# Hybrid decoder layer on one core: resident shared-expert weights, moved routing tables, merged list products

## The chip, the cores and the metric

The kernel runs on one core of a Trainium2 chip. Its time is the device time of one execution in microseconds (us); lower is better. The engines are PE (TensorE, matrix products into PSUM), DVE (VectorE), ACT (ScalarE), POOL (GpSimd) and SP (SyncE, which issues most transfers). All transfers run on 16 DMA engines that the queues of SP, ACT and POOL share.

## The reference

One decoder layer for 512 tokens of width 1024, all in f32. After the token mixers the layer computes a shared expert and 8 of 64 routed experts for each token:

```python
h2 = rmsnorm(x, g_ffn)
idx, wts = route(h2, w_router, router_bias)   # sigmoid scores, top 4 of 8 groups, top 8 of 64 experts
moe = routed_experts(h2, idx, wts, w_exp_gate, w_exp_up, w_exp_down) \
    + swiglu(h2, w_sh_gate, w_sh_up, w_sh_down)
x = x + moe
x = x + sigmoid(rmsnorm(x, g_ple) @ w_ple_gate) * rmsnorm(p @ w_ple_proj, g_ple_post)
```

`swiglu(x, wg, wu, wd)` is `(silu(x @ wg) * (x @ wu)) @ wd`. Gate and up weights, shared or of one expert, are 1024 x 256 (1 MiB each), down weights 256 x 1024 (1 MiB).

## The kernel before, in words

**Memory.** `ring` has 12 slots of 8 KB for each partition, 1 MiB each. It holds the dense weights of the mixers first (`DENSE`, `DENSE_SLOT`), then the experts: the four experts of a group take three slots each, from slot 9, 0, 3 and 6 on (`EXPERT_SLOT`; gate, up, down). `gates` holds the mixers' gates, 16 chunks of 512; once the branches are merged into its first half `lo`, the second half `hi` is free. Before the change `hi` then takes the gain row `gffn`, the per-layer inputs `prow`, the router weights `rw` and the scratch of the selection (`choice`, `masked`, `repl`, `gscr`).

**Stages.** Query, key, value and pool products, attention and gates run to 208 us; the two branches and their merge to 265 us; the output projection, second norm, router and selection of the four 128-token tiles interleave from 263 to 349 us (PE's order is written out by hand: `out_proj`, `second_T`, `router`, `rank`, with pieces of `shared_up` as filler); then 40 row steps to 909 us; then the rows are summed and the last gate applied.

**Row steps.** A list of (token, expert) pairs is built for each group of four experts: `place` is a one-hot matrix of list slots, bf16, made by DVE (`places`). PE multiplies it with two tables: `tokc` (token index in two exact bf16 parts, `list_rows`, 2 columns wide) and `tokw` (three bf16 parts of the weight and the rank, 4 columns for each of two experts, `list_weights`, 8 columns wide). Groups 0 to 7 have lists of 96 rows for each expert and take three steps of 128 rows, groups 8 to 15 have 64 and take two. The lists of group r are made in step r, for r from 1 to 15, between the row transposes and the down product; the weights of group 0 join in step 1.

A step r is on PE: gate and up products of 128 gathered rows (L2105, four strips of 32 rows with an expert each), transposes of the activations of step r-1 (L2114), transposes of the rows of step r+1 (`rows_T`, L1654), `lists(r)`, then the down product of step r-1 (L2134). POOL gathers rows from `h2_rows` in HBM and scatters weighted results to `accumulator`, 0.5 MiB each way for a full step. The first gather waits until all of `h2_rows` is stored by ACT's queue (L900), and until the first row list is there. PE's order before the first step is: two pieces of a shared product, `rows_T(0)`, the last four k of `shared_up(1)`, then `up(0)`.

**SP's queue.** Loads are issued in program order, each behind a wait for its slot. `load_group(g)` loads group g while group g-1 is computed: gate and up of position 0 after step 0 of the group, of position 1 after step 1, of positions 2 and 3 after step 2 (L500), and the down weights behind the down products (L519). In front of the loop stand the weights of experts 0 to 3; gate and up of expert 3 are the last, after `shared_ps` has reached 2.

**The shared expert.** `shared_up` computes gate and up of tiles 0 and 1 ahead of the loop, from ring slots 6 and 7. Those slots are then needed for expert 3, so the same weights are loaded a second time, into pieces of `gates` (`shg_late`, `shu_late`, L547 and L549), for tiles 2 and 3, which are computed in steps 24 to 26 (`late_up`: eight products 256 wide for gate and eight for up). SP issues the second load after the first gather has landed (L546).

## Time and profile before

| | |
|---|---|
| time, median of 3 runs (lowest to highest) | 996.4 us (994.88 to 996.63) |
| profiled execution: its time, its span | 995.38 us, 993.5 us |
| busy: PE, DVE, ACT, POOL | 941.1, 339.4, 162.6, 201.4 us |
| moved by DMA | 301.03 MB, 303 GB/s over the span |
| mean granted TensorE clock | 0.986 of full |

Some times of the profiled execution around the change, from its timeline: SP issued gate and up of expert 2 at 327.5 us; DVE ended the last gain product at 330.3; ACT issued the last store of h2 rows at 332.3; DVE ended the last masked weights at 336.5; POOL issued the first gather at 338.8; SP issued gate and up of expert 3 at 349.6; PE began the first row step at 349.3. The transfers that SP issued from 343.4 to 371.2 are, in order: the shared gate (1 MiB), the shared up in two halves (1 MiB), the post gain (0.5 MiB), gate and up of expert 3 (2 MiB), gate and up of position 0 of group 1 (2 MiB), the two halves of the per-layer projection (1 MiB), gate and up of position 1 (2 MiB) and the down weights of position 0 (1 MiB).

How to read it: the span runs from the first to the last instruction, the execution's time is some 2 us longer. Busy times overlap between engines. An idle engine costs something only where the chain runs through it.

### The profile page before, as it was taken

To read this page: it belongs to the slowest core of one execution; us is meant where nothing else is said; L and a number is where in the kernel's file an instruction comes from. 1 tells how busy PE (TensorE), PEld (TensorE's weight loads), DVE (VectorE), ACT (ScalarE), POOL (GpSimd) and SP (SyncE) were. 2 spreads that over 40 slices of the span, in tenths; PEclk is the share of its full clock that TensorE was granted. 3 is DMA by queue.
4 is the path that set the end of the run, shared out by engine and by line. 5 is a ranking of instruction groups with operands and counts; after the bars stand their busy time and mean duration, and the time that the engine had idled before them with its cause. 6 is when DMAs were issued, how large, how long until landed. Compare 5 with 4: busy or idle time off the path is not lost.

```text
span 993.5 us, 15496 instructions
## 1 busy us (share of the span) xinstructions
PE 941.1 (95%) x6263; PEld 465.7 (47%) x6263; DVE 339.4 (34%) x749; ACT 162.6 (16%) x304; POOL 201.4 (20%) x332
## 2 busy tenths in 40 slices
PE   6999999999999999999999999999979898997698
PEld 4578888854446533333333333354323332332344
DVE  5565673222226753333332111111101111111687
ACT  2001334120011211111111111111101112121021
POOL 4115923000010102222222222212121211101210
PEclk9999999999999999999999999999989999999799
DMA  9940002265362599999999999999999999999972
GB/s 331 326 128 1 1 1 85 85 201 180 105 288 75 195 385 373 410 416 401 393 418 415 414 419 414 410 423 415 405 422 422 422 420 421 414 400 361 368 274 84
DMA packets 83911, 301.03 MB, mean 303 GB/s; under 512 B 9299, under 2 KB 35959, under 8 KB 59648
## 3 DMA queue, kind: packets, MB, share of 16 engines
q1 hardware_dynamic: 71200, 264.24, 67.7%
q0 software_dynamic: 11920, 33.63, 8.7%
q10 hardware_dynamic: 720, 2.16, 0.5%
q8 instruction: 50, 0.82, 0.3%
q14 instruction: 21, 0.17, 0.0%
HBM read 279.26 MB, written 29.36 MB: 311 GB/s over the span
## 4 chain that ended last, share of the span: by engine, by line
PE 76%; DMA 18%; DVE 2%; SPq 2%; issue 1%; ACT 1%; DVEq 0%; POOL 0%; ACTq 0%
PE ps L2105 22%; DMA ring<-in_w_exp_up 16%; PE ps L1721 12%; PE ps L2134 9%; PE ps L1860 6%; PE ps L2247 5%; PE ps L1677 3%; PE ps L1844 3%; PE ps L1842 3%; PE ps L1654 2%; DMA ring<-in_w_exp_down 2%; PE ps L1931 1%; PE ps L1683 1%; PE ps L2114 1%; SPq L514 1%; SPq L500 1%
## 5 line engine op out<-in xcount | busy, mean ns | idle before, releaser
L2105 PE MATMUL ps<-ring,gates 128*32 128x512 f32 x2560 | 288.8, 603 | 26.1 <-DMA ring<-in_w_exp_up 25.4
L2105 PEld LDWEIGHTS ps<-ring,gates 128*32 128x32 f32 x2560 | 87.6, 111 | 219.0 <-issue 218.1
L2134 PE MATMUL ps<-ring,poolbuf 128*32 128x512 f32 x1280 | 147.3, 601 | 3.0 <-DMA ring<-in_w_exp_down 2.1
L1482 DVE COPY poolbuf<-ps 128x256 f32<-128x256 f32 x40 | 17.0, 424 | 356.2 <-PE ps L2114 356.2
L747 POOL TENSOR_TENSOR tickets<-cst 128x1 f32<-128x1 f32 x77 | 14.5, 188 | 398.2 <-ACT actT L946 392.7
L2134 PEld LDWEIGHTS ps<-ring,poolbuf 128*32 128x32 f32 x1280 | 38.3, 110 | 84.7 <-issue 83.0
L946 ACT ACTIVATE actT<-ps,qT 128x1024 f32<-128x1024 f32 x40 | 44.5, 1113 | 143.9 <-PE ps L2134 143.9
L938 ACT ACTIVATE poolbuf<-ps 128x256 f32<-128x256 f32 x40 | 15.3, 384 | 279.3 <-PE ps L2105 279.3
L1721 PE MATMUL ps<-xrow,ring 128*128 128x256 f32 x256 | 57.9, 381 | 0.1
L1860 PE MATMUL ps<-ring,gates 128*128 128x512 f32 x128 | 56.4, 594 | 0.0
L1654 PE MATMUL ps<-cst,rows 128*128 128x128 f32 x352 | 48.5, 285 | 7.6 <-DVE rows L1035 7.6
L1721 PEld LDWEIGHTS ps<-xrow,ring 128*128 128x128 f32 x256 | 48.3, 190 | 8.0 <-issue 1.2
L1654 PEld LDWEIGHTS ps<-cst,rows 128*128 128x128 f32 x352 | 44.7, 193 | 9.5 <-issue 8.9
L1721 PE MATMUL ps<-actT,ring 128*128 128x256 f32 x208 | 47.5, 381 | 0.0
L688 POOL TENSOR_SCALAR st<-st 128x1 f32<-128x1 f32 (+2 forms) x17 | 6.7, 393 | 196.2 <-ACT rows L891 135.3
L759 POOL DMA_INDIRECT rows<-h_rows,stage x40 | 41.8, 1045 | 21.4 <-issue 19.0
L764 POOL DMA_INDIRECT accumulator<-actT,stage x40 | 40.6, 1016 | 22.1 <-issue 22.1
L2247 PE MATMUL ps<-ring,actT 128*128 128x512 f32 (+1 forms) x112 | 42.2, 531 | 0.0
L1721 PEld LDWEIGHTS ps<-actT,ring 128*128 128x128 f32 x208 | 39.0, 190 | 6.7 <-issue 1.4
L720 POOL TENSOR_TENSOR ring<-ring 128x1024 f32<-128x1024 f32 x12 | 28.3, 2361 | 52.4 <-DMA ring<-in_w_gate 30.3
L1860 PEld LDWEIGHTS ps<-ring,gates 128*128 128x128 f32 x128 | 23.8, 190 | 27.3 <-issue 27.3
L2247 PEld LDWEIGHTS ps<-ring,actT 128*128 128x128 f32 x112 | 20.9, 190 | 18.0 <-issue 17.2
(269 smaller groups left out, 1001.3 us busy)
## 6 DMA issues: line engine op xcount, KB each, us to landing
ring<-in_w_exp_down SPq DMA_DIRECT2D x64, 1024.0 KB
ring<-in_w_exp_gate SPq DMA_DIRECT2D x62, 1024.0 KB, 10.8
ring<-in_w_exp_up SPq DMA_DIRECT2D x62, 1024.0 KB, 18.9
ring<-accumulator SPq DMA_DIRECT2D x12, 1024.0 KB, 12.5
ring<-in_w_gate SPq DMA_DIRECT2D x8, 1024.0 KB, 10.1
ring<-in_w_in SPq DMA_DIRECT2D x5, 1024.0 KB, 13.0
xrow<-in_x SPq DMA_DIRECT2D x8, 512.0 KB, 7.5
accumulator<-ring SPq DMA_DIRECT2D x1, 4096.0 KB, 19.6
```

The source lines that it names most:

```text
L759: pool.indirect_dma_start(hg[j], None, h2_dram, bass.IndirectOffsetOnAxis(ap=stage[:, 0, j, :], axis=0), bounds_check=T - 1, oob_is_err=Fa ...
L764: pool.indirect_dma_start(y_dram, bass.IndirectOffsetOnAxis(ap=stage[:, 1, j, :], axis=0), yrow[j], None, bounds_check=ACC_ROWS - 1, oob_i ...
L946: nc.scalar.activation(yrow[j], bank(6, 2), ACT.Copy, scale=slot_wr[:, r, 0:1]).then_inc(y_ready, 1)
L1654: last = nc.tensor.transpose(bank(b0 + half)[:, k * width:(k + 1) * width], v[0:width, 4 * half + k, :], ident[0:width, 0:width])
L1677: last = mm(bank(2 * (i % 2)), actT[:, k, i * P:(i + 1) * P], qv[:, k], start=(k == 0), stop=(k == KD - 1))
L1721: last = mm(out[:, f * HALF_T:(f + 1) * HALF_T], w[:, k, f * P:(f + 1) * P], x[:, k, :], start=(k == 0), stop=(k == 3))
L1842: mm(bank(b), wa[:, k, mi * P:(mi + 1) * P], mixedT[:, k, :], start=(k == 0), stop=(k == 3))
L1844: last = mm(bank(b + 1), wb[:, k, mi * P:(mi + 1) * P], qT[:, k, :], start=(k == 0), stop=(k == 3))
L1860: last = mm(bank(half), gates[:, k, i * P:(i + 1) * P], w[:, k], start=(k == 0), stop=(k == KD - 1))
L2105: last = mm(bank(2 + k)[part, :], hgT[k][:, q, part], pair_view(EXPERT_SLOT[js[c]])[:, q], start=(q == 0), stop=(q == KD - 1))
L2134: last = mm(bank(6 + half)[part, :], eactT[r % 2][:, q, part], w[:, q, half * 512:(half + 1) * 512], start=(q == 0), stop=(q == 1))
L2247: last = mm(gate_bank(i, n0)[:, 0:width], xT, unit_view(s, 4)[:, k % 4, n0 % 512:n0 % 512 + width], start=(k == 0), stop=(k == KD - 1))
```

## The change

The first load of the shared gate and up weights goes into all of `hi` (`w_sh`), behind the routing tables, and stays there for all four tiles; the second load is gone. The routing tables take ring slots 6 and 7: `gffn` and `prow` slot 6, `rw` and the selection's scratch slot 7. So expert 3's gate weights (slot 6) are loaded once the gain products and the transposes of `prow` are done, and its up weights (slot 7) once the selection's masked weights are there; neither waits for the first gather or for `shared_ps`. `gpost` is loaded ahead of both. The shared activations `sh_row` move to the last quarter of `lo`.

`tokw` gets six columns for each expert: the two of `tokc`, copied in once, and the four it had. One product of 12 columns (`list_all`) takes the place of `list_rows` and `list_weights`; only the first list of group 0 is still made from `tokc` alone (`first_rows`). `late_up` makes eight products 512 wide. An unused identity copy (`idT`) is dropped.

```diff
@@ -53,7 +53,8 @@
 TCOL, WCOL = 2, 4
-LCOL = TCOL + 2 * WCOL
+ECOL = TCOL + WCOL
+LCOL = 2 * ECOL
 LATE = (2, 3)
@@ -148,8 +149,8 @@
 DENSE = ["q0", "q1", "kv", "pool0", "pool1"] + [f"gate{p + h * PAIRS}" for p in range(PAIRS) for h in range(2)] + \
-    ["wa0", "wb0", "wa1", "wb1"] + [f"out{c}" for c in range(4)] + ["shg", "shu"]
-DENSE_SLOT = [u % 8 for u in range(17)] + [1, 2, 3, 4, 6, 7]
+    ["wa0", "wb0", "wa1", "wb1"] + [f"out{c}" for c in range(4)]
+DENSE_SLOT = [u % 8 for u in range(17)] + [1, 2, 3, 4]
 DENSE_AT = {name: n for n, name in enumerate(DENSE)}
@@ -224,19 +225,17 @@
         pp = hi.rearrange("p (i n) -> p i n", i=NT)
-        prow = hi[:, 2 * D:3 * D].rearrange("p (i n) -> p i n", i=NT)
-        rw = hi[:, 3 * D:3 * D + KD * NE].rearrange("p (k e) -> p k e", k=KD)
-        gffn = hi[:, 0:D]
-        sh_row = hi[:, 0:NT * FE].rearrange("p (i f) -> p i f", i=NT)
+        gffn = ring[:, 6, 0:D]
+        prow = ring[:, 6, D:2 * D].rearrange("p (i n) -> p i n", i=NT)
+        rw = ring[:, 7, 0:KD * NE].rearrange("p (k e) -> p k e", k=KD)
+        w_sh = hi.rearrange("p (u k n) -> p k u n", u=2, k=KD)
+        sh_row = lo[:, 3 * D:4 * D].rearrange("p (i f) -> p i f", i=NT)
         sh_act = hi[:, 2 * T:4 * T].rearrange("p (j n) -> p j n", j=2)
...
         NR = NT * NE
-        lo3 = lo[:, 3 * D:4 * D]
         rows3 = rows[:, 3, :]
-        shg_late = hi[:, 2 * D:4 * D].rearrange("p (k n) -> p k n", k=KD)
-        shu_late = [w.rearrange("p (k n) -> p k n", k=KD // 2) for w in (lo3, hi[:, D:2 * D])]
-        choice, masked, repl, gscr = (hi[:, D + k * NR:D + (k + 1) * NR] for k in range(4))
+        choice, masked, repl, gscr = (ring[:, 7, KD * NE + k * NR:KD * NE + (k + 1) * NR] for k in range(4))
         key_row, above, perm = (poolbuf[0:NE, PL + k * NE:PL + (k + 1) * NE] for k in range(3))
@@ -250,7 +249,7 @@
         ka = kT[:, :, :].rearrange("p a n -> p (a n)")
-        WM = NR * WCOL // 2
+        WM = NR * ECOL // 2
         tokw = ka[:, 0:WM].bitcast(BF16).rearrange("p (i e c) -> p i e c", i=NT, e=NE)
@@ -264,7 +263,6 @@
         oneT = sb("oneT", [P, P], BF16)
-        idT = sb("idT", [P, P], BF16)
         order = vecs[0:1, 0:NE].bitcast(U32)
@@ -313,7 +311,7 @@
         x1_ps, x1_ready = sem("x1_ps"), sem("x1_ready")
-        mid_loaded, late_loaded, sh_late_loaded = sem("mid_loaded"), sem("late_loaded"), sem("sh_late_loaded")
+        mid_loaded, late_loaded, shared_loaded = sem("mid_loaded"), sem("late_loaded"), sem("shared_loaded")
         ssq2_done, rstd2_ready, xg_ready, h2_ready, act_moved = (
@@ -369,10 +367,6 @@
                 return t["w_out"][0].rearrange("(k p) n -> p k n", p=P)[:, :, n * 256:(n + 1) * 256]
-            if name == "shg":
-                return t["w_sh_gate"][0].rearrange("(k p) n -> p k n", p=P)
-            if name == "shu":
-                return t["w_sh_up"][0].rearrange("(k p) n -> p k n", p=P)
             raise ValueError(name)
@@ -481,18 +475,19 @@
             sp.dma_start(y_rows[0], zero_row.unsqueeze(1).broadcast_to([P, TOPK, D])).then_inc(y_first, 16)
-            for u in range(8, DENSE_AT["shg"]):
+            for u in range(8, N_DENSE):
                 load_dense(u)
...
                 sp.dma_start(xrow[:, i, :], x_rows[i]).then_inc(x_loaded[i], 16)
-            for u in range(DENSE_AT["shg"], N_DENSE):
-                load_dense(u)
             sp.wait_ge(merged_ready, KD)
...
             sp.dma_start(rbias, t["router_bias"].broadcast_to([P, NE])).then_inc(mid_loaded, 16)
+            for u, name in enumerate(("w_sh_gate", "w_sh_up")):
+                sp.dma_start(w_sh[:, :, u, :], t[name][0].rearrange("(k p) n -> p k n", p=P)
+                             ).then_inc(shared_loaded, 16)
@@ -540,16 +535,13 @@
             load_in(2, 2)
+            sp.dma_start(gpost, t["g_ple_post"].broadcast_to([P, D])).then_inc(late_loaded, 16)
+            sp.wait_ge(xg_ready, 2 * NT)
+            sp.wait_ge(pT_ps, 2)
+            load_part(3, 3, 0)
             sp.wait_ge(logit_ps, NT)
-            sp.wait_ge(pT_ps, 2)
-            sp.wait_ge(sel_ready, NT)
-            sp.wait_ge(gathered[0], 16)
-            sp.dma_start(shg_late, unit_source("shg")).then_inc(sh_late_loaded, 16)
-            for c in range(2):
-                sp.dma_start(shu_late[c], unit_source("shu")[:, 4 * c:4 * c + 4, :]).then_inc(sh_late_loaded, 16)
-            sp.dma_start(gpost, t["g_ple_post"].broadcast_to([P, D])).then_inc(late_loaded, 16)
-            sp.wait_ge(shared_ps, 2)
-            load_in(3, 3)
+            sp.wait_ge(masked_ready, 2)
+            load_part(3, 3, 1)
             sp.wait_ge(order_ready, 1)
@@ -1055,7 +1047,6 @@
             nc.vector.memset(oneT[:, :], 1.0)
-            nc.vector.tensor_copy(idT[:, :], cst[:, C_ID:C_ID + P])
@@ -1310,6 +1301,10 @@
             nc.vector.tensor_copy(tokc[:, :, 1], cst[:, C_TILE:C_TILE + NT])
+            nc.vector.tensor_copy(tokw[:, :, :, 0],
+                                  cst[:, C_PM:C_PM + 1].unsqueeze(1).broadcast_to([P, NT, NE]))
+            nc.vector.tensor_copy(tokw[:, :, :, 1],
+                                  cst[:, C_TILE:C_TILE + NT].unsqueeze(2).broadcast_to([P, NT, NE]))
             residual(0, 0)
@@ -1409,11 +1404,11 @@
             tw3 = tokw.rearrange("p i e c -> p (i e) c")
-            link(nc.vector.tensor_copy(tw3[:, :, 0], r_w))
-            link(nc.vector.tensor_tensor(rest, r_w, tw3[:, :, 0], ALU.subtract))
-            link(nc.vector.tensor_copy(tw3[:, :, 1], rest))
-            link(nc.vector.tensor_tensor(rest, rest, tw3[:, :, 1], ALU.subtract))
-            nc.vector.tensor_copy(tw3[:, :, 2], rest)
+            link(nc.vector.tensor_copy(tw3[:, :, TCOL], r_w))
+            link(nc.vector.tensor_tensor(rest, r_w, tw3[:, :, TCOL], ALU.subtract))
+            link(nc.vector.tensor_copy(tw3[:, :, TCOL + 1], rest))
+            link(nc.vector.tensor_tensor(rest, rest, tw3[:, :, TCOL + 1], ALU.subtract))
+            nc.vector.tensor_copy(tw3[:, :, TCOL + 2], rest)
@@ -1424,7 +1419,7 @@
                 b, span = 1 - b, 2 * span
-            nc.vector.tensor_scalar(tokw[:, :, :, 3], count_of[:, b, :, HEAD:], -1.0, None, ALU.add
+            nc.vector.tensor_scalar(tokw[:, :, :, TCOL + 3], count_of[:, b, :, HEAD:], -1.0, None, ALU.add
                                     ).then_inc(tokw_ready, 1)
@@ -1434,7 +1429,7 @@
                 r = slice(FIRST_STEP[g], FIRST_STEP[g] + n)
-                w = found[:, :, TCOL:].rearrange("p s (e c) -> p s e c", e=2)
+                w = found.rearrange("p s (e c) -> p s e c", e=2)[:, :, :, TCOL:]
                 own = cst[:, C_PAIR:C_PAIR + 6] if g < BIG_GROUPS else cst[:, C_PAIR2:C_PAIR2 + 4]
@@ -1909,26 +1904,17 @@
-                i = LATE[c]
-                pe.wait_ge(sh_late_loaded, 48)
                 pe.wait_ge(h2T_ready, 2 * NT + 2 * c + 2)
                 for k in range(KD):
-                    xT = xT_late[k // 4][:, k % 4, :]
-                    mm(bank(5)[:, 0:FE], xT, shg_late[:, k, :], start=(k == 0), stop=(k == KD - 1))
-                for k in range(KD):
-                    xT = xT_late[k // 4][:, k % 4, :]
-                    last = mm(bank(5)[:, FE:2 * FE], xT, shu_late[k // 4][:, k % 4, :], start=(k == 0),
-                              stop=(k == KD - 1))
+                    last = mm(bank(5), xT_late[k // 4][:, k % 4, :], w_sh[:, k], start=(k == 0), stop=(k == KD - 1))
                 last.then_inc(shared_ps, 1)
...
                 if i == 0 and k0 == 0:
-                    loaded("shg")
-                    loaded("shu")
-                w = pair_view(DENSE_SLOT[DENSE_AT["shg"]])
+                    pe.wait_ge(shared_loaded, 32)
                 for k in range(k0, k1):
-                    last = mm(bank(SH_BANK[i]), actT[:, k, i * P:(i + 1) * P], w[:, k], start=(k == 0),
+                    last = mm(bank(SH_BANK[i]), actT[:, k, i * P:(i + 1) * P], w_sh[:, k], start=(k == 0),
                               stop=(k == KD - 1))
@@ -1982,13 +1968,14 @@
-            def list_rows(g, at, s):
+            def first_rows(at, s):
                 for i in range(NT):
-                    last = mm(at, place[:, g % 2, i, s * P:(s + 1) * P], tokc[:, i, :], start=(i == 0),
+                    last = mm(at, place[:, 0, i, s * P:(s + 1) * P], tokc[:, i, :], start=(i == 0),
                               stop=(i == NT - 1))
...
-            def list_weights(g, at, s):
+            def list_all(g, s):
+                at = bank(5)[:, (g % 2) * 64 + s * LCOL:(g % 2) * 64 + (s + 1) * LCOL]
                 e = g * GROUP + pair_of(g, s)
@@ -1997,7 +1984,7 @@
             for s in range(steps_of(0)):
-                last = list_rows(0, bank(5)[:, 328 + s * TCOL:328 + (s + 1) * TCOL], s)
+                last = first_rows(bank(5)[:, 328 + s * TCOL:328 + (s + 1) * TCOL], s)
             last.then_inc(list_ps, 1)
@@ -2025,13 +2012,11 @@
                     for s in range(steps_of(0)):
-                        list_weights(0, bank(5)[:, s * LCOL + TCOL:(s + 1) * LCOL], s)
+                        list_all(0, s)
                 else:
...
                 for s in range(steps_of(g)):
-                    at = (g % 2) * 64 + s * LCOL
-                    list_rows(g, bank(5)[:, at:at + TCOL], s)
-                    last = list_weights(g, bank(5)[:, at + TCOL:at + LCOL], s)
+                    last = list_all(g, s)
                 last.then_inc(list_ps, 1)
@@ -2190,9 +2175,7 @@
                 for i in range(NT):
-                    mm(bank(5)[0:CAP, 0:TCOL], o_place[:, i, :], tokc[:, i, :], start=(i == 0), stop=(i == NT - 1))
-                for i in range(NT):
-                    last = mm(bank(5)[0:CAP, TCOL:TCOL + WCOL], o_place[:, i, :],
+                    last = mm(bank(5)[0:CAP, 0:ECOL], o_place[:, i, :],
                               tokw[:, i, bass.ds(e, 1), :].rearrange("p e c -> p (e c)"),
```

## Rows read from the trace of the kernel before

**Rows 1.** The page: busy time of the engines, and DMA share in 40 slices.
```profile
PE 941.1 (95%) x6263; PEld 465.7 (47%) x6263; DVE 339.4 (34%) x749; ACT 162.6 (16%) x304; POOL 201.4 (20%) x332
...
DMA  9940002265362599999999999999999999999972
```

**Rows 2.** Windows: us, busy of PE, PEld, DVE, ACT, POOL, clock, DMA share, GB/s.
```profile
336.00:339.00 3.00, 3.00 (x27) 1.67 (x26) 1.91 (x11) 0.01 (x1) 0.39 (x2) 1.00 0.02 5
336.00:378.00 42.00, 41.27 (x347) 18.09 (x346) 20.01 (x69) 7.46 (x12) 8.30 (x16) 1.00 0.83 307
357.00:378.00 21.00, 20.27 (x211) 8.02 (x211) 6.43 (x24) 2.69 (x4) 4.46 (x10) 1.00 0.98 380
366.00:577.00 211.00, 211.00 (x2144) 81.75 (x2146) 66.65 (x243) 36.21 (x52) 49.67 (x106) 1.00 1.00 405
585.00:903.00 318.00, 290.64 (x2272) 112.76 (x2270) 43.83 (x86) 48.34 (x79) 53.66 (x114) 0.98 1.01 415
```

**Rows 3.** Waits of PE from 349 to 910 us.
```profile
PE ps L2105 <- DMA ring<-in_w_exp_up: 25.4, 14, 4.3
```

**Rows 4.** The chain that ended last, in order: start, us, what.
```profile
378.32 1.12 PE ps L1654 x8
...
390.89 0.90 PE ps L1654 x8
391.79 0.08 PE ps L1987 x4
391.87 0.10 PE ps L1994 x4
...
392.38 3.57 PE ps L2134 x32
...
585.19 16.91 DMA ring<-in_w_exp_up
```

**Rows 5.** Timeline of SyncE's queue: first and last of 13 issues.
```profile
343.42 0.38 SPq L547 DMA_DIRECT2D gates<-in_w_sh_gate  x1
...
371.15 0.33 SPq L519 DMA_DIRECT2D ring<-in_w_exp_down  x1
```

**Rows 6.** Windows: groups of experts, and single microseconds.
```profile
378.00:415.00 37.00, 37.00 (x390) 14.56 (x390) 13.63 (x45) 6.29 (x9) 8.48 (x18) 1.00 0.99 399
452.00:489.00 37.00, 37.00 (x374) 14.55 (x371) 11.68 (x45) 6.58 (x10) 8.47 (x18) 1.00 1.01 408
561.00:597.00 36.00, 36.00 (x325) 13.38 (x326) 4.34 (x10) 6.66 (x10) 8.48 (x18) 1.00 1.01 414
379.00:380.00 1.00, 1.00 (x32) 0.97 (x35) 0.73 (x2) 0.53 (x1) 0.00 (x0) 1.00 0.83 242
416.00:417.00 1.00, 1.00 (x32) 0.97 (x30) 0.98 (x3) 0.50 (x1) 0.00 (x0) 1.00 1.00 324
597.00:598.00 1.00, 1.00 (x14) 0.58 (x16) 1.00 (x3) 0.40 (x1) 0.00 (x0) 1.00 1.02 418
```

**Rows 7.** The store of h2 rows, issued at 281.7 and at 332.3.
```profile
L900 ACTq DMA_DIRECT2D h_rows<-rows x1: 339/339/339, 281.7 to 281.7; - x1
...
DMA to landing us min/median/max: 8.0/8.0/8.0
...
DMA to landing us min/median/max: 3.7/3.7/3.7
```

**Rows 8.** Timeline of POOL before the loop.
```profile
337.75 0.18 POOL L752 COPY stage<-qT 128x1 uint32<-128x1 uint32 x1 [7.07 <-DVE qT L1364]
338.80 1.19 POOL L759 DMA_INDIRECT rows<-h_rows,stage  x1 [0.86 <-POOL stage L752]
```

**Rows 9.** Timeline of PE's weight loads: the first of the transposes.
```profile
344.42 0.19 PEld L1654 LDWEIGHTS ps<-cst,rows 128*128 128x128 f32 x1 [0.24 <-issue]
```

**Rows 10.** The third gather, issued at 343.0: us to landing.
```profile
DMA to landing us min/median/max: 7.6/7.6/7.6
```

**Rows 11.** Timeline of DVE: a cast of 256 columns.
```profile
348.18 0.46 DVE L1412 CAST kT<-qT 128x256 bf16<-128x256 f32 x1
```

## The prediction

> **What bounds the kernel now.** I read the page first: PE is busy 95% of the span and the DMA engines sit at 9 tenths in nearly every slice from the 15th on [rows 1], so both look like the bound. The windows by stage part them. Between 366 and 577 us PE is busy every microsecond while DMA moves 405 GB/s; between 585 and 903 us PE is busy 290.6 of 318 us and DMA moves 415 GB/s [rows 2]. The list of waits says what PE missed there: 25.4 us in 14 waits for gate/up weights [rows 3], and the chain first hands over from PE to such a transfer at 585.19 [rows 4]. So the routing stage and the first 20 or so of the 40 row steps are bound by PE's own work, the rest by the weight stream, and the tail after 903 follows it.
>
> The 99% of DMA share before 585 needs a second look, because it decides what saved bytes are worth. The queue is empty at 336 to 339 us (5 GB/s) [rows 2]. From there to 378 us SyncE issues 13 transfers of 10.5 MiB, 11.0 MB the first and the last in [rows 5], and GpSimd four gathers of 0.52 MB: 13.1 MB. Moved in 336 to 378: 307 GB/s x 42 us = 12.9 MB [rows 2]. So at 378, with the late shared weights in it, the stream has caught up: some 0.2 MB open. The same shows just after the two-expert loads that each group's third step releases: the microsecond from 379 moves 242 GB/s, and the one from 416 moves 324, but the one from 597 moves 418 [rows 6]. Until about 490 us the stream lives from hand to mouth: PE frees a slot, and only then is there something to move.
>
> **The change part by part.**
>
> *2 MiB less to load.* The late copies of the shared gate and up weights (three transfers from 343.4 on [rows 5]) go. They are 2.1 MB, which at the 380 to 415 GB/s of [rows 2] is 5.1 to 5.5 us of stream. What hides them is the empty queue before and the catch-up by 378; PE waits for no transfer before 585. I take 0. Without that cover it would be 5.5 us.
>
> *Expert 3's gate and up earlier* (from 349.6 to about 330.3 and 336.5, where the second gain product and the last mask end). Another 2.1 MB leave the loaded stretch, also worth 0: from 357 to 378 the stream will idle some 5 us and be just as caught up.
>
> *First copy of the shared weights.* It moves behind the router loads at 265 us; its first product is some 60 us later. The 6 MiB of expert weights behind it end a few us later than now, and the first step at 349 us is the first to need them. 0 us.
>
> *List products merged.* Each of a step's two products (four matmuls with a 128x128 stationary, 2 and 8 columns wide) becomes one of 12 columns. In the chain four take 0.08 us 2 wide and 0.10 us 8 wide [rows 4]: width hardly counts, so I price 12 wide as the average. Per product group: 24 matmuls become 12 where a group has three steps, 16 become 8 where it has two, 36 become 24 at the first. Removed: 12 x 7 + 8 x 8 = 148. From the chain: 391.79 to 392.38 is 0.59 us for 24 [rows 4], 24.6 ns each, so 148 x 24.6 = 3.6 us (if a 12 wide product cost a quarter more than an 8 wide one, 0.10 to 0.125 us for four, 1.0 us less). They lie on PE's chain at steps 1 to 15, all before 550 us, where nothing hides them. The Trainium skill (TensorE: Matmul & The Clock Gate, LDWEIGHTS) has a load of a stationary of 128 columns take about 107 ns; by an estimate from that page alone the 148 would be worth 15.8 us. The 0.10 us for four loads and products in [rows 4] speaks against it, and the measurement decides.
>
> *Can the stream follow?* A group moves 399 x 37 = 14.8 to 414 x 36 = 14.9 MB [rows 6], at 415 GB/s 35.9 us. PE's group falls from 37.0 to 36.1 us (two groups), from 36.4 to 35.8 (two), then stays 35.25. The stream loses 0.1 us in each of the second two, nothing in the first two: it follows, and the saving survives to 585 and from there to the end, for behind 585 nothing is changed. The other bound: at the 408 GB/s of 452 to 489 [rows 6] a group takes 36.5 us, 0.4 + 0.4 + 0.7 + 0.7 = 2.2 us of the 3.6 are lost. I take the first, because 408 was moved with a queue that ran dry, so it is demand, not capacity.
>
> *What is now in front of the first gather.* SyncE no longer waits for the first gather before it loads. In its queue after 327.5 stand 2 MiB (expert 2), 0.5 MiB (the post gain, moved up), 1 MiB (expert 3 gate, 330.3) and, from 336.5, 1 MiB more; on ScalarE's queue the last 0.5 MiB of h2 rows, issued at 332.3. The first four are 4.2 MB; begun at 329 and moved at 415 GB/s [rows 2] they end at 339.1, the fifth at 341.6. In the kernel before this store landed 3.7 us after issue, with the last of expert 2 beside it; the one of 281.7, in the midst of the 6 MiB of expert weights, took 8.0 us [rows 7]. The second is the like case: 332.3 + 8.0 = 340.3 instead of 336.0. All gathers wait for it. The stage copy is now at 337.75, set by the row list, and the gather issues 1.05 us later [rows 8]; then 340.4 + 1.05 = 341.45. It landed by 343.4 (SyncE's next issue behind its wait [rows 5]), 4.6 us after issue; then 346.0. PE wants the rows at 344.4 [rows 9], and behind that transpose stand the last four shared products and the first step. Stall: 1.6 us. Bounds: 0 if the store lands before 337.4; if it lands only with the fifth transfer (341.6) the gather issues at 342.8 and lands at 347.4 to 350.4 (4.6, or 7.6 like the third gather, which ran beside the late loads [rows 10]): 3.0 to 6.0 us.
>
> *Small.* The gather of step 3 lands beside less traffic: its transposes took 1.12 us at 378.32 against 0.90 at 390.89 [rows 4], so 0.2 us back. Two DVE copies of 256 bf16 (0.46 us each, by a cast of that size [rows 11]) fall behind the last merge at 265 us, where DVE waits for the output projection; without that cover 0.9 us. The late shared product keeps its columns (8 products of 512 for 16 of 256): 0, and it lies in the weight-bound part. The dropped identity copy: below 0.3 us, under PE's first products: 0.
>
> Sum against the profiled execution (995.38 us, span 993.5): -3.6 - 0.2 + 1.6 = -2.2, so 993.2. That execution lies 1.0 us under the median of 996.4, within their scatter; against the median the forecast is 994.2 us.
>
> **Rivals.**
>
> B. *No stall.* The Trainium skill (DMA: Bandwidth & Descriptors, Queues, rings and completion order) says that each DMA engine takes turns between queues packet by packet. As a mechanism here: the 0.5 MiB store moves at half of 415 GB/s beside the weights, 1.3 us longer than alone, so with the 3.7 us of [rows 7] it lands at 337.3, just before the row list. Then there is no stall, -3.8: 992.6. The 8.0 us of 281.7 speak against it.
>
> C. *The stream bounds from the start*, as the DMA row of the page suggests. Then the merged products are hidden, but the 4.2 MB that leave the loaded stretch count in full: 5.5 + 5.1 = 10.6 us, 985.8. The caught-up queue at 378 and the dips speak against it.
>
> D. *The first gather is held.* It decides from a landing at 350.2 on: 344.4 + 3.8 (what the rest saves) + 2.0. At the bound of 350.4 the stall is 6.0 and the time 996.4 - 3.8 + 6.0 = 998.6, slower. It takes the store behind the fifth transfer and a slow gather together in one queue.
>
> E. *The saving is lost in the stream.* 408 GB/s is what it can do; 3.6 shrinks to 1.4, and with the stall of 1.6 nothing is left: 996.4.
>
> **How the numbers follow.** A, the forecast, 0.40; B 0.20; C 0.07; E 0.23; D 0.10. A measurement of this kernel can tell about 0.2%, 2.0 us, from no change, and A lies on that edge: with its stall of 0.5 to 2.5 us it reads 993.1 to 995.1, six tenths of it faster. Faster: 0.24 + 0.20 + 0.07 = 0.51; the rest of A less 0.03, and E, are same: 0.36; slower 0.10 + 0.03 = 0.13. The range takes in A, B, E and the lower half of D, with 1.2 us for scatter: 991.5 to 997.6.
>
> **What would show it.** Merged products: at step 3 the stretch from the last row transpose to the down product falls from 0.59 to 0.30 us. Bytes: 301.0 to 298.9 MB in total; DMA share in 357 to 378 near 0.75 instead of 0.98 with no gain from it. Stall: the landing of the fourth h2 store (3.7 to about 8 us), the first gather's issue (338.8 to 341.4) and an idle gap of PE before its transposes at 345. Follow: PE's first wait for weights still near step 20. The prediction is wrong if the first row step starts more than 3 us after 349.3, if PE waits for weights before step 15, or if dips as at 379 are gone with the time much shorter (C).

## The result: 0.28% slower

| | before | after |
|---|---|---|
| time, median (lowest to highest) | 996.08 us (994.48 to 997.25, 8 runs) | 999.57 us (996.57 to 1000.01, 8 runs) |
| profiled execution: span | 993.5 us | 998.1 us |

The ratio is 1.0028, 95% interval 1.0018 to 1.0037: 2.8 us slower by the ratio and 3.5 us by the two medians, where 2.2 us faster was forecast, and outside the range. Of the rivals, E had the merged products right (their saving is lost in the stream), and D the way the time moved and, at its mild end, the path of the stall; the stall was larger than E or the forecast put it.

### The profile page after: what moved, and what is told of

Its sections match the earlier page's. It is cut to its first block, busy times and chain, and to the rows that moved or that the text cites. A ratio compares the mean times of both kernels' runs of the same rounds, so it can differ in the third digit from the quotient of the medians.

```text
span 998.1 us, 15132 instructions
## 1 busy us (share of the span) xinstructions
PE 937.9 (94%) x6083; PEld 457.1 (46%) x6083; DVE 340.5 (34%) x750; ACT 162.8 (16%) x304; POOL 199.2 (20%) x332
## 4 chain that ended last, share of the span: by engine, by line
PE 72%; DMA 22%; SPq 3%; DVE 1%; issue 1%; ACT 1%; POOL 0%; POOLq 0%; ACTq 0%
PE ps L2090 22%; DMA ring<-in_w_exp_up 18%; PE ps L1716 12%; PE ps L2119 8%; PE ps L1855 6%; PE ps L2230 4%; PE ps L1672 3%; PE ps L1839 3%; PE ps L1837 3%; PE ps L1649 2%; SPq L438 2%; PE ps L1909 1%; PE ps L1678 1%; PE ps L2099 1%; DMA ring<-accumulator 1%
## 5 line engine op out<-in xcount | busy, mean ns | idle before, releaser
L2090 PE MATMUL ps<-ring,gates 128*32 128x512 f32 x2560 | 287.8, 602 | 31.6 <-DMA ring<-in_w_exp_up 30.9
L680 POOL TENSOR_SCALAR st<-st 128x1 f32<-128x1 f32 (+2 forms) x17 | 4.7, 278 | 196.5 <-ACT rows L883 135.6
```

What stands on the lines that cost most here:

```text
L2090: last = mm(bank(2 + k)[part, :], hgT[k][:, q, part], pair_view(EXPERT_SLOT[js[c]])[:, q], start=(q == 0), stop=(q == KD - 1))
```

## The profile after

The page of the changed kernel, its busy time and its bytes, answers to [rows 1]:

```profile
PE 937.9 (94%) x6083; PEld 457.1 (46%) x6083; DVE 340.5 (34%) x750; ACT 162.8 (16%) x304; POOL 199.2 (20%) x332
...
DMA packets 81814, 298.91 MB, mean 299 GB/s; under 512 B 9251, under 2 KB 33863, under 8 KB 57552
```

PE works 3.2 us less and 2.1 MB fewer are moved, both as forecast. The span is 4.6 us longer all the same. The chain that ended last says where it starts (start, us, what):

```profile
332.37 9.14 DMA h_rows<-rows
341.51 0.06 issue
341.57 0.20 POOL stage L744
...
342.62 4.60 DMA rows<-h_rows,stage
347.21 0.04 issue
347.26 1.97 PE ps L1649 x8
349.23 4.26 PE ps L1917 x8
353.49 2.69 PE ps L2090 x21
```

The last store of h2 rows takes 9.14 us, against 3.7 in [rows 7]. POOL copies the row list the moment it has landed, so the list is not what is late; the gather goes out at 342.62, against 338.80 in [rows 8]. The eight transposes of PE begin at 347.26, and the first row step at 353.4; it was 349.3 before. The windows around that stretch (columns as in [rows 2]) show a second loss on top of the wait:

```profile
345.00:347.00 2.00, 0.08 (x1) 0.00 (x0) 1.93 (x5) 0.00 (x0) 1.23 (x3) 1.00 0.63 217
347.00:349.00 2.00, 1.74 (x8) 1.75 (x9) 1.79 (x7) 0.59 (x1) 0.83 (x1) 0.59 0.69 180
349.00:351.00 2.00, 2.00 (x5) 0.91 (x4) 1.90 (x4) 0.61 (x2) 0.00 (x0) 0.56 0.26 94
351.00:353.00 2.00, 2.00 (x6) 0.76 (x4) 1.90 (x7) 0.00 (x0) 0.00 (x0) 1.00 0.00 0
```

PE idles from 345, and for the 4 us after that the granted clock is 0.59 and 0.56, near its 1.2 GHz level, before it is full again. Eight transposes take 1.97 us and the last four k of the shared product 4.26; the variant `hold` below has 0.88 and 3.44 at full clock. So 353.49 against that variant's 349.31 is 2.27 us of waiting, 1.09 of slow transposes and 0.82 of slow products. Not all of the 1.09 is the clock: in `up_late` and `split` below the same eight transposes take 1.15 us behind a wait with the clock at full, so 0.27 us come with the wait and 1.64 us with the clock.

Later stretches of the same kernel, and PE's waits from 320 to 910 us (total, times, longest):

```profile
357.00:378.00 21.00, 20.27 (x206) 8.12 (x200) 6.52 (x24) 3.08 (x5) 2.76 (x6) 1.00 0.72 274
366.00:577.00 211.00, 208.58 (x2008) 79.33 (x2004) 65.83 (x243) 36.03 (x52) 49.88 (x106) 1.00 1.00 402
585.00:903.00 318.00, 289.53 (x2244) 106.51 (x2240) 43.12 (x84) 48.38 (x78) 54.90 (x116) 0.98 1.01 415
```

```profile
PE ps L2090 <- DMA ring<-in_w_exp_up: 30.9, 14, 5.6
PE ps L1649 <- DMA rows<-h_rows,stage: 2.2, 1, 2.2
```

From 357 to 378 the share is 0.72 (0.98 in [rows 2]): the stream has slack there, and it buys nothing. Behind 585 the rate is the same 415 GB/s. PE's waits for gate and up weights grow from 25.4 us [rows 3] to 30.9. Two places in the chain show the merged products and what took them back:

```profile
382.17 0.90 PE ps L1649 x8
383.07 0.28 PE ps L1981 x12
383.35 3.57 PE ps L2119 x32
```

```profile
514.38 18.62 DMA ring<-in_w_exp_up
533.00 0.14 issue
533.13 3.16 PE ps L2090 x25
```

Twelve products lie between the last transpose and the down product, 0.28 us instead of the 0.59 of [rows 4]. But PE's first wait for weights has moved from 585 us [rows 4] (the transfer that step 21 waits for) up to step 15.

The timelines give the start of each row step. This table carries most of what follows (us; `hold` and the others are the experiments below; `half_before2` and `half_hold` are the kernel before and `hold` with the list layout `half`):

| step | before | after | hold | lists | double | half_before2 | half_hold |
|---|---|---|---|---|---|---|---|
| 0 | 349.27 | 353.42 | 349.24 | 349.31 | 349.38 | 349.10 | 349.34 |
| 8 | 445.11 | 446.94 | 442.74 | 442.93 | 449.15 | 444.69 | 442.85 |
| 14 | 517.92 | 518.58 | 514.38 | 516.22 | 524.35 | 517.49 | 514.49 |
| 15 | 530.05 | 533.13 | 529.03 | 529.44 | 536.88 | 529.62 | 526.70 |
| 20 | 589.19 | 592.13 | 589.70 | 589.42 | 596.43 | 588.77 | 585.78 |
| 21 | 602.24 | 606.29 | 601.91 | 603.29 | 608.18 | 600.52 | 597.53 |
| 30 | 740.71 | 745.80 | 741.18 | 742.23 | 745.59 | 737.20 | 736.99 |
| 39 | 892.48 | 896.91 | 892.19 | 893.39 | 896.36 | 888.33 | 887.28 |

After against before: 4.15 us behind at step 0, only 0.66 behind at step 14, so 3.5 us gained by the lists; 3.08 behind again one step later, 4.05 at step 21 and 4.43 at step 39.

## The experiments

The question is twofold: is the late gather the whole of the loss, and who takes the 3.5 us of the lists. Each median stands beside one of the kernel before from the same chip; those lie from 995.3 to 997.1 us, so kernels of different chips are compared by their ratios.

### The late gather

**hold.** The changed kernel, with the wait for the first gather put back ahead of the post gain and expert 3.

```diff
+            sp.wait_ge(gathered[0], 16)
             sp.dma_start(gpost, t["g_ple_post"].broadcast_to([P, D])).then_inc(late_loaded, 16)
             sp.wait_ge(xg_ready, 2 * NT)
```

> The changed kernel, with SyncE waiting for the first gather before it loads the post gain and expert 3, as the kernel before does. Theory S (the loss is the late store of h2 rows and the first gather behind it; behind the first row step the stream sets the end in both kernels, so merged products and the 2 MiB less give nothing): store lands 3.7 us after issue, first gather issues at 338.8, first row step starts at 349.4 and the time is that of the kernel before within 1 us, about 996. Rival P (the saving of the merged products reaches the end, and the loss at the start hid it): first step at 349.4 and the time about 992.5, 3.6 us under before. Rival Q (the loss is elsewhere): first step later than 351 and the time near 999.6.

Measured 995.10 us, ratio 0.9999 [0.9986, 1.0011]. The same stretch of its chain:

```profile
343.08 1.91 PE ps L1918 x4
344.99 0.88 PE ps L1650 x8
345.87 3.44 PE ps L1918 x8
349.31 4.84 PE ps L2091 x41
```

No transfer is in it, and the store lands in 3.9 us. With the post gain and expert 3 loaded late again the whole loss is gone, so it comes from the loads in front of the gather. And all else of the change together is worth nothing, within 1.4 us, though it has the lists, the 2 MiB less and the moved tables in it.

**fill.** The store and the gather stay late; PE does the rest of the shared product first.

```diff
-            rows_T(0)
             shared_up(1, 4, 8)
+            rows_T(0)
```

> The changed kernel, with the last four k of the second shared product (3.4 us) ahead of the transposes of the first gathered rows instead of behind them; all loads as in the changed kernel. Store and gather stay late (341.5 and 347.2), but PE has work in its gap and its clock should not fall: transposes at 348.3, first row step at about 350.5. Theory S: time about 3.0 us under the changed kernel, 996.6. If the first step starts at 350.5 and the time stays at 999.6, the start does not set the end.

Measured 995.98 us, 1.0008 [0.9997, 1.0019]. From 345 to 347 us PE is busy all the time, and the clock stays full:

```profile
345.00:347.00 2.00, 2.00 (x6) 0.81 (x5) 1.93 (x5) 0.00 (x0) 1.23 (x2) 1.00 0.71 199
```

Step 0 begins at 350.12, 0.85 us late instead of 4.15. The 2.2 us of waiting and the slow clock behind it are thus the loss, and the 3.4 us of shared products that stood behind the transposes are enough to cover most of them.

**up_late.** Only the second half of expert 3 (its up weights) is held until the gather has landed.

```diff
             load_part(3, 3, 0)
             sp.wait_ge(logit_ps, NT)
             sp.wait_ge(masked_ready, 2)
+            sp.wait_ge(gathered[0], 16)
             load_part(3, 3, 1)
```

> The changed kernel, with only the up weights of expert 3 held until the first gather has landed; the post gain and expert 3's gate weights stay ahead of the last store of h2 rows. If the store waits for what was queued before it and beside it, it lands near 339.5 instead of 341.5, the gather issues near 340.7 and lands near 345.3; the first step starts near 350.5 and the time is some 3 us under the changed kernel. If only what stands ahead of the store counts, it lands at 341.5 as before and nothing is gained.

Measured 997.59 us, 1.0016 [1.0003, 1.0030].

```profile
332.42 8.63 DMA h_rows<-rows
...
342.16 4.59 DMA rows<-h_rows,stage
...
346.80 1.15 PE ps L1650 x8
347.94 3.44 PE ps L1918 x8
351.38 2.69 PE ps L2091 x21
```

The store takes 8.63 instead of 9.14 us. With the loads of the changed kernel as they are it took 8.4 us in `fill` and 8.9 in `spread_after` (below), 9.1 in the changed kernel and 10.0 in `split`, so the last 1 MiB, issued 4 us behind it, shows no effect beyond that scatter. The delay comes with what stands ahead of the store: the 2 MiB of expert 2 are there in `hold` too, where it took 3.9 us, which leaves the 1.5 MiB that are new. Which part of these counts, post gain or gate weights, no run separates. PE idled 1.7 us here and the clock stayed full, and 353.49 - 351.38 = 2.1 us come back, 1.64 of them from the clock. The expected 3 us are not there.

**split.** The changed kernel with each merged list product parted again (2 and 10 columns).

```diff
-                    last = mm(at, place[...], tokw[...], start=(i == 0), stop=(i == NT - 1))
+                    mm(at[:, 0:TCOL], place[...], tokc[:, i, :], start=(i == 0), stop=(i == NT - 1))
+                for i in range(NT):
+                    last = mm(at[:, TCOL:], place[...], tokw[...][:, TCOL:], start=(i == 0), stop=(i == NT - 1))
```

> The changed kernel, with each list product split in two again (148 matmuls more, 2 and 10 columns wide). Theory S: time like the changed kernel, 999.6, since the end follows the first step's start (353.5) and the stream. Rival P: the saving is real and only masked: 3.6 us over the changed kernel, 1003.

Measured 997.64 us, 1.0026 [1.0016, 1.0036]: the same ratio as the changed kernel's 1.0028, so the merged products give nothing there. This run also bears on the clock. Its store took 10.02 us and PE waited 3.0 us for the gather, longer than in the changed kernel, but the clock did not fall:

```profile
347.00:349.00 2.00, 0.85 (x7) 0.85 (x8) 1.80 (x6) 0.10 (x1) 1.23 (x2) 1.00 0.65 176
349.00:351.00 2.00, 2.00 (x8) 1.04 (x7) 1.89 (x4) 0.99 (x2) 0.10 (x1) 1.00 0.58 168
```

Its first step began at 352.67. In `spread_after`, the changed kernel with another layout of the lists (below), PE waited only 1.9 us at this place, and the clock did fall:

```profile
347.00:349.00 2.00, 2.00 (x10) 1.48 (x11) 1.79 (x7) 1.20 (x2) 0.74 (x1) 0.67 0.53 158
349.00:351.00 2.00, 2.00 (x4) 0.91 (x3) 1.90 (x4) 0.00 (x0) 0.00 (x0) 0.50 0.35 104
```

So the clock fell in two of four profiled executions with a late gather, and how much of it is in the median of the changed kernel is not shown. Without it the first row step is 2.5 (changed kernel, 4.2 - 1.64) to 3.4 us (`split`) late.

### Where the saving of the lists goes

**lists.** The kernel before with the merged products alone (the wider `tokw`, `list_all` instead of two products).

```diff
-LCOL = TCOL + 2 * WCOL
+ECOL = TCOL + WCOL
+LCOL = 2 * ECOL
...
-                    list_rows(g, bank(5)[:, at:at + TCOL], s)
-                    last = list_weights(g, bank(5)[:, at + TCOL:at + LCOL], s)
+                    last = list_all(g, s)
```

> The kernel before, with only the list products merged (six-column table, 148 matmuls fewer). Theory S: PE's steps 1 to 15 are 0.2 to 0.3 us shorter each, but PE's first wait for weights comes near step 15 instead of step 21 and takes it back: time within 1 us of before. Rival P: 3.6 us less.

Measured 996.14 us, 0.9998 [0.9985, 1.0012]. The 3.6 us are not there even alone. Up to step 8 this kernel is 2.2 us ahead, at step 20 0.2 behind. Its waits from 349 to 540 us, a stretch in which the kernel before has none for weights:

```profile
PE ps L2109 <- DMA ring<-in_w_exp_up: 2.5, 2, 1.4
```

In `hold` the same happens in one place. It is 3.54 us ahead at step 14, as the 148 matmuls by 24.6 ns said; then this:

```profile
510.19 18.71 DMA ring<-in_w_exp_up
528.89 0.14 issue
529.03 3.25 PE ps L2091 x13
```

The 64 gate and up products of step 15 in `hold` and in the kernel before (start, us) show that the wait of 2.5 us isn't all of it:

```profile
529.03 8.77 PE L2091 MATMUL ps<-ring,gates 128*32 128x512 f32 x64 [2.51 <-DMA ring<-in_w_exp_up]
530.05 7.05 PE L2105 MATMUL ps<-ring,gates 128*32 128x512 f32 x64
```

Behind the wait the granted clock is 0.50 from 530 to 532 us, and the products take 1.7 us longer. So of the 3.54 us `hold` loses 2.5 to the wait and 1.7 to the clock, and step 20 begins 0.5 us behind. In `lists` the clock stays full (its step 12 waits 1.4 us, step 15 1.1, step 18 0.8), and the lead is lost all the same. That the wait comes early is no accident of one execution: the changed kernel, `hold`, `fill` and `hold_pad` wait first at step 15, `lists` and `up_late` at step 12, while none of the eight kernels with separate products and the old list layout waits for weights before step 18.

**double.** The kernel before with all list products of groups 1 to 15 made twice: the edit with its sign turned.

```diff
                     at = (g % 2) * 64 + s * LCOL
                     list_rows(g, bank(5)[:, at:at + TCOL], s)
+                    list_rows(g, bank(5)[:, at:at + TCOL], s)
+                    list_weights(g, bank(5)[:, at + TCOL:at + LCOL], s)
```

> The kernel before, with each list product of steps 1 to 15 made twice (296 matmuls more, 7.2 us of PE). If PE's steps 1 to 15 set the end: 7.2 us more. If the stream of weights already runs at its limit from the first step on (theory S), the part that PE's steps are below the stream's pace is free: 2 to 4.5 us more, and PE's first wait for weights comes after step 21.

Measured 999.23 us, 1.0035 [1.0021, 1.0048]. At step 20 it is 7.24 us behind, every microsecond of the added work; at step 39 only 3.88. Half of what PE loses in the first 20 steps is given back behind them. It waits for weights less there (23.7 us instead of 25.4), which accounts for half of what is given back, and for the first time at step 25. So neither removed nor added work of these steps reaches the end in full.

**half2 and half10.** The kernel before, with the gate and up weights of group 2, or of group 10, loaded by half (4.2 MB less; the other half of the slots keeps old weights, so the outputs are not the reference's).

```diff
+                col = slice(0, UNIT // 2 if less[0] else UNIT)
-                sp.dma_start(ring[:, s, :], (exp_gate, exp_up)[n][...]
+                sp.dma_start(ring[:, s, col], (exp_gate, exp_up)[n][...][:, col]
...
+                less[0] = g == 2        # or 10
```

> The kernel before, with only the first half of each gate and up load of group 2 made (4.2 MB less, issued between 403 and 441 us; the other half of those weights is stale). 10 us of stream at 415 GB/s. PE is bound by its own work there, so the queue should run empty and the gain be kept only as far as the stream was behind: 0 to 2 us. If the stream binds from the first step on with nothing to spare, more: up to the 4 us that PE's steps can be ahead.

> The kernel before, with only the first half of each gate and up load of group 10 made (4.2 MB less, in the stretch where PE waits for weights; the other half is stale). The stream sets the end: 10 us less, 4.2 MB at 415 GB/s.

Measured 994.88 us, 0.9984 [0.9970, 0.9997], and 989.40 us, 0.9931 [0.9915, 0.9948]. The same 4.2 MB are worth 1.6 us early and 6.9 us late. At 415 GB/s they are 10.1 us of transfer, so even late 3 us less than expected. Early bytes are nearly free, and the 2 MiB that the change no longer loads, earlier still, fit that. The profiled execution of `half10` waits 2.1 us for weights at step 18, ahead of its edit (the loads of group 10 are issued from step 26 on), so the first wait of the kernel before need not be at step 21 in every execution.

### What the stream is limited by

**pad and hold_pad.** Empty list slots gather row 511 instead of nothing (4.2 MB more), on the kernel before and on `hold`.

```diff
-                nc.vector.tensor_tensor(from_row[:, r], tile_of, found[:, :, 0], ALU.add)...
+                nc.vector.tensor_scalar(from_row[:, r], row_of[:, r], float(T - 1), None, ALU.min)...
```

> The kernel before, with the row index of an empty list slot set to 511 instead of one that the gather skips: 1024 more rows of 4 KB are gathered (4.2 MB more over the loop; the rows are not used). Theory I (what binds the stream is the most loaded of the 16 DMA engines, those whose slots are always full; the others have gaps where slots are empty): the extra rows fall to engines with time to spare and cost little, under 3 us. Theory M (the engines' mean binds): 4.2 MB at 415 GB/s, about 10 us more, less what lies before step 20 (about half): 5 to 10 us.

> The changed kernel with SyncE waiting for the first gather (as in the run hold), and in addition row 511 gathered for every empty slot (4.2 MB more). Theory I: PE's first wait is still at step 15 and the time is 0 to 3 us over hold. Theory M: the stream has 12 GB/s less to spare in steps 3 to 15, so PE waits at step 12 or before, and the time is 4 us or more over hold.

Measured 997.50 us, 1.0022 [1.0009, 1.0035], and 997.62 us, 1.0025 [1.0016, 1.0034]. From 500 to 585 us `pad` moves more than `hold` and never waits, while `hold` moves less and does (one window of each, `pad` first):

```profile
500.00:585.00 85.00, 85.00 (x818) 31.95 (x811) 19.18 (x72) 15.01 (x22) 19.78 (x42) 1.00 1.02 420
```

```profile
500.00:585.00 85.00, 82.49 (x753) 29.53 (x741) 17.22 (x63) 13.69 (x19) 19.86 (x42) 0.98 0.99 399
```

With PE waiting, 399 GB/s go through where 420 can. Part of that is the wait's own doing, since a late PE frees slots late. The stretch that ends with the landing of step 15's weights is nearly free of it (`hold` first, then `hold_pad`):

```profile
390.00:529.00 139.00, 136.52 (x1323) 51.77 (x1322) 48.83 (x180) 24.89 (x36) 31.70 (x68) 1.00 1.01 415
390.00:529.00 139.00, 136.89 (x1324) 52.23 (x1323) 48.93 (x180) 25.08 (x36) 31.27 (x67) 1.00 1.02 420
```

`hold` moves 415 GB/s here, the very capacity of the prediction, with a DMA share of 1.01, and the weights are 2.5 us late. `hold_pad` moves 420 and waits 2.6 us at the same step. A rate averaged over a stretch is therefore not what decides about the wait.

**skip_odd and skip_high.** The kernel before, whose gathers leave out the odd partitions, or partitions 64 to 127: 8.4 MB less each (rows not gathered keep old data, so the outputs are not the reference's).

```diff
+                nc.vector.tensor_scalar(from_row[:, r], row_of[:, r], cst[:, C_SKIP:C_SKIP + 1], None, ALU.add)...
...
+    c[:, C_SKIP] = T * (p % 2)        # or T * (p >= P // 2)
```

> The kernel before, with the gather skipping every odd partition's row (about 2048 of 4096 rows, 8.4 MB less; those rows keep what an earlier gather left). To be read beside the next kernel, which skips as many rows. Theory M (the engines' mean sets the stream): both gain alike, by what lies behind step 20, some 1000 rows or 4.2 MB, 10 us. Theory I (the most loaded engine sets it): the two differ, since one of the two patterns takes whole engines out of the gather and leaves the others with all their rows, and that one gains nearly nothing, the other 10 us or more.

> The kernel before, with the gather skipping partitions 64 to 127 (about 2048 of 4096 rows, 8.4 MB less). Theory M: the same gain as with the odd rows skipped, 10 us. Theory I: if rows go to the engines in runs of neighbouring partitions, half the engines keep all their rows and the gain is near 0; if they go round the engines, this one gains 10 us and the odd one near 0.

Measured 980.29 us, 0.9846 [0.9832, 0.9860], and 1000.33 us, 1.0042 [1.0028, 1.0056]. Fewer bytes make it 15 us faster or 4 us slower, by where in the tile they are missing. That the two differ is what theory I expected and theory M did not; `pad` and `hold_pad`, at 2.2 and 2.5 us, cost less than M wanted too.

**Three layouts of the lists.** The empty slots of a list lie at its end. These kernels give slot s another rank; the rows moved are the same (on the kernel before the unused identity copy is dropped as well, to make room for the table).

```diff
-                low, cap = CAP - cap_of(g) + 1, cap_of(g)
+                cap = cap_of(g)
+                at = C_SPREAD if g < BIG_GROUPS else C_SPREAD2
...
+        c[:, at:at + cap] = CAP - cap + 1 + (r % 8) * (cap // 8) + r // 8    # spread
+        c[:, at:at + cap] = CAP - cap + 1 + (cap - 1 - s)                    # reverse
+        c[:, at:at + cap] = CAP - cap + 1 + (s % 2) * (cap // 2) + s // 2    # half
```

`spread` gives each run of 8 slots the same number of empty ones, `reverse` puts them first, `half` puts the lower half of a list on even slots and the upper half on odd ones. The "variant with the two holds" of the expectations is `hold`: one wait, which holds the post gain and expert 3.

> The kernel before, with the ranks of an expert's list laid over its slots in another order: slot r holds rank (r mod 8) x 12 + r div 8 (by 8 for the small groups), so that each run of 8 partitions has as many empty slots as any other. Nothing else is moved, the rows are the same (the unused identity copy makes room for the table). Theory I: every engine has about 0.8 of its row slots to move instead of some all: a two-step group falls from 34.7 to about 34.0 us, three-step groups come under PE's pace, PE's first wait for weights comes after step 24: 5 to 10 us less, 986 to 991. Theory M: no change.

> The changed kernel with SyncE waiting for the first gather (run hold), and ranks laid over the slots as in the run before this one. Theory I: 5 to 10 us less than hold, and, since the stream no longer takes it back by step 15, part or all of the 3.6 us of the merged products besides: 0 to 3.6 us under the run before this one. Theory M: 995, as hold.

> The changed kernel as it is, with the ranks laid over the slots in the same way. It still has the late store and gather, first step at 353.4. Theory S and I: 3 to 4 us over spread_hold.

> The variant with the two holds on SP's queue (995.1 us), and the ranks of each list laid over its slots in reverse, so that the empty slots lie at the list's start instead of its end. The same rows are moved, and rows that are neighbours in the list stay neighbours. Theory I (what counts is how many full slots the most loaded DMA engine has, an engine serving a run of 8 consecutive slots): the load is only mirrored, 995 us (+-1.5). Theory II (the spread layout cost 8 us because neighbours in the list no longer lie side by side): neighbours still lie side by side, 995 us too. Theory III (any layout in which the filled slots do not come first costs time): about 1000 to 1004 us.

> The same variant with the lower half of each list on the even slots and the upper half on the odd ones, so that side by side lie rows that are 48 (or 32) places apart in the list; the empty slots are the odd ones at the list's end. Theory I (most loaded engine, runs of 8 slots): the first runs of 8 are still full, so 995 us (+-1.5). Theory II (neighbours): no two neighbours of the list lie side by side, about 1003 us, as in the spread layout (1004.5). Theory III: about 1000 to 1004 us here and in the reversed layout both.

> The kernel before with nothing changed but the layout of the lists (lower half of a list on the even slots, upper half on the odd ones). The same layout on the variant with the two holds gave 989.2 us, and there the merged list products kept their lead: step 20 began 3.4 us before that of the kernel before. If PE sets the time where the stream is relieved (the prediction's own reason), the two separate products cost here what they were predicted to cost, 148 matmuls by 24.6 ns, so 989.2 + 3.6 = 992.8 us (+-1.5), and no step up to 20 waits for weights. If the layout alone gives the gain and the stream still sets the time, the merged products are worth nothing here too: 989.2 us (+-1.5), with the first weight wait later than in the variant with the holds.

| kernel | median, us | ratio |
|---|---|---|
| before + spread | 1004.74 | 1.0086 [1.0064, 1.0107] |
| hold + spread | 1004.49 | 1.0085 [1.0064, 1.0106] |
| after + spread | 1006.46 | 1.0103 [1.0080, 1.0126] |
| hold + reverse | 994.18 | 0.9979 [0.9967, 0.9990] |
| hold + half | 989.16 | 0.9913 [0.9894, 0.9932] |
| before + half | 990.93 | 0.9950 [0.9938, 0.9963] |

The theory behind `spread`, that the most loaded DMA engine sets the pace and serves runs of 8 slots, wanted a gain and got 8 us of loss. The theory of near neighbours wanted the same loss for `half`; it gained 6. Theory III wanted a loss for `reverse`; it lost nothing. All three have fallen in this form. What is left is the fact that the order of the same rows in a tile moves the time by 15 us. One rival is left untested: only the run of 8 is contradicted, not the most loaded engine. By its formula `spread` gathers the empty slots at the last places of each 8 (slots 6 and 7, as long as a quarter of a list or less is empty), so every first run of 4 is full. If an engine served runs of 4 slots, which no trace here shows, the loss of `spread` and the gain of `half` and `skip_odd` could be what theory I wants; the 4 us of loss of `skip_high` would still stand against it.

`half` answers the question about the lists, though. Here is a stretch of `hold` + `half`, the same as above for `hold`:

```profile
500.00:585.00 85.00, 84.93 (x790) 31.50 (x786) 18.69 (x68) 14.67 (x21) 19.77 (x42) 1.00 1.01 418
```

With the stream relieved, PE does not wait at steps 15 and 16, and step 20 begins at 585.78, against 588.77 with `half` on the kernel before: the lists' lead, 3.0 us, is alive there. It is taken back further on. At step 25 both kernels start at 649 us (649.45 and 649.06), at step 39 1.05 us are left, and 0.6 us of the spans (987.8 and 988.4). So of the last expectation neither case came in full. The layout gives 5.8 us of its own by the medians of one chip, 5.0 by the ratio. `hold` + `half` is faster than that by 0.6 us of the profiled spans, 1.8 by the medians and 3.7 by the ratios, whose intervals do not overlap. How much of the merged products is alive at the end with this layout is therefore open, between nothing much and all of it; the difference also holds the rest of the change.

## Why the prediction was wrong

**The merged list products**: the term of 3.6 us was right as PE work. 24 matmuls in 0.59 us became 12 in 0.28, and `hold` is 3.54 us ahead at step 14. On the price of a weight load the Trainium skill (TensorE: Matmul & The Clock Gate, LDWEIGHTS) would have given 15.8 us, as estimated from it in the prediction; the measurement is against it as a price in a chain. In the trace of the kernel before one such load lasts 96 ns (L1987, median of 140), near the figure of the Trainium skill, but the loads overlap: 24 loads with their products took 0.59 us.

**The step that failed** is "it follows, and the saving survives to 585 and from there to the end". It put the saving at -3.6; it is 0 in `lists` and in `hold`, within 1.5 us. The argument took the rates of [rows 6] as demand and 415 GB/s as capacity, and compared means over groups of 36 us. `hold` moved 415 up to step 15 and `pad` 420, so the number was not wrong; what was wrong is that a mean decides. In `hold` the weights of step 15 landed 18.7 us after their issue at 510.19, and PE was ready for them at 526.5, 16.3 us after. In the kernel before the same load was issued at 513.53 and needed at 530.05, 16.5 us after, and was there by then: `hold` issues it 3.3 us earlier, and its landing at 528.89 is only 1.2 us ahead of 530.05. So with its lead PE reaches the edge of the stream at step 15, not at step 21. A second term was at nothing without a reason: behind such a wait the clock can fall, which took 1.7 us of the 3.54 in `hold`. The prediction also had the sign in its own rows: with 25.4 us of waits for weights behind 585 [rows 3], a PE that arrives earlier there only waits longer, unless the stream too is ahead. `double` and `half10` fit this from either side. Rival E had it at 0.23, with 1.4 us left of the saving; none is seen. Its reason, a capacity of 408 GB/s, is not what the runs show.

The balance that found the stream caught up at 378 was short as well: GpSimd had issued five gathers by then (338.80, 341.00, 342.99, 368.93, 375.28) and a scatter (373.19), not four gathers, so up to 1.2 MB were open and not 0.2.

**The stall** was mis-sized. The mechanism was the predicted one, step for step, each 1.2 us later: the store landed at 341.5 (340.3 forecast), the gather went at 342.6 (341.45) and landed at 347.2 (346.0). PE waited 2.2 us where the forecast had 1.6. What no step had is the clock: in the profiled execution 1.64 us more went to a clock of 0.56 to 0.59 behind the wait, so the first row step was 4.15 us late, and the prediction's own sign of being wrong, more than 3 us, came. `fill` and `hold` give the loss back. This is the lower bound of rival D (gather out at 342.8, landed at 347.4), which had put it down to the fifth transfer; `up_late` shows no effect of that one. Rival B, no stall, rested on the rule of the Trainium skill (DMA: Bandwidth & Descriptors, Queues, rings and completion order) that queues take turns packet by packet; a store that needs 9.14 us instead of 3.7 disagrees with the half share worked out from it.

**What was right**: 2 MiB less for nothing (total 298.9 MB, share 0.72 from 357 to 378, where 0.75 was forecast), and against C, which counted those bytes in full. That the later first copy of the shared weights costs nothing is seen only in `hold`, together with the rest. Expert 3 early saved nothing, as forecast, but with the post gain it made the store late.

Sum as it came: 0 for the lists, 0 for the bytes, and the stall, 2.5 to 4.15 us at the first row step, to the end: +3.5 us by the medians, +2.8 by the ratio.

**Open**: what limits the stream, and with it why the landing of step 15's weights does not come earlier in `hold`. Bytes, mean rate, an engine serving runs of 8 slots, and neighbouring rows are each contradicted by a run. The number of packets is too: it is 83911 in the kernel before, `pad`, `skip_odd` and `skip_high` alike. How rows of a gather are shared out over the 16 DMA engines would be the next thing to measure; the trace as read here does not name the engine of a packet. Also open is how often the clock falls behind a wait.

## What to carry to other kernels

Here, work taken off an engine that later waits for a stream moved the waits forward and not the end. Before counting it, ask how long the loads behind the next waits take from issue to landing, and how soon they are needed; a rate averaged over a stage doesn't tell. Loads moved ahead of a store that something waits for were paid for there: hold them back, or put work that is ready in front of the waiting instruction (`fill`, one line moved, was worth 2.0 us by the ratios, 3.6 by the medians). And the order of rows in an indirect transfer is a thing to try for itself: with `half` it was worth 5 to 6 us, more than the whole change. Of the kernels that gather every row the fastest is `hold` + `half`, 0.9913 [0.9894, 0.9932] of the kernel before.

## What the runs showed of the hardware that was not expected

The same count of gathered rows left out made the kernel 15.3 us faster (odd partitions) or 4.2 us slower (upper half). The same rows in other slots gave 1004.5, 994.2 or 989.2 us. Of four executions in which PE waited 1.7, 1.9, 2.2 and 3.0 us for the first gather, those with 1.9 and 2.2 us fell to a granted clock of 0.50 to 0.67 afterwards, the others not. At step 15 the clock fell behind waits of 2.5 us (`hold`), 2.6 (`hold_pad`) and 2.7 (`fill`), and not behind 2.4 us in the changed kernel. A 0.5 MiB store took 3.7 to 3.9 us with 2 MiB issued ahead of it on SyncE's queue (kernel before, `hold`), and 8.4 to 10.0 us with 3.5 MiB.
